# A new order of work between two attentions, and ScalarE copying both halves of the first attention's keys and values out of PSUM

## The reference, cut to what matters

```
h = rms_norm(x, attn_norm_w);  z = h @ w_in
c_q, c_kv, k_rope, dq, dk, dv, g_mla, g_diff = split_columns(z)
o_mla  = mla_attention(q(c_q), k(c_kv, k_rope), v(c_kv))          # 16 heads
o_diff = diff_attention(norm(dq), norm(dk), dv, lam, alibi)        # 8 heads, a1 - lam * a2
o_diff = rms_norm(o_diff, diff_subln_w) * (1 - lam_init)           # per head of 128
merged = sigmoid(g_mla + b) * o_mla + sigmoid(g_diff + b) * o_diff
x = x + merged @ w_out
x = x + expert_choice_moe(rms_norm(x, ffn_norm_w), ...)            # 16 experts
```

## Time and profile before

| | |
|---|---|
| median of the runs | 1512.5 us |
| the profiled execution: its time, and its span from the first to the last instruction | 1515.71 us, 1514.0 us |
| PE busy | 1162.2 us (77%) |
| DVE, ACT, POOL busy | 510.4, 373.4, 48.9 us |
| chain that ended last | DMA 53%, PE 39%, DVE 5%, ACT 1% |
| granted PE clock, mean | 0.88 of full speed |

### The profile page before, as it was taken

One profiled execution on the slowest core, in us unless ns is written; L12 is line 12 of the kernel. 1 busy time (PEld: TensorE's weight loads), 2 busy tenths in 40 slices (PEclk: granted clock), 3 DMA queues, 4 the chain that ended last, 5 costly groups with the idle time before them and its releaser, 6 DMA issues.

```text
span 1514.0 us, 19783 instructions
## 1 busy us (share of the span) xinstructions
PE 1162.2 (77%) x8185; PEld 693.2 (46%) x8185; DVE 510.4 (34%) x945; ACT 373.4 (25%) x616; POOL 48.9 (3%) x78
## 2 busy tenths in 40 slices
PE   9999899876557666566666666666665999999998
PEld 8877688422112112112122122122121778999887
DVE  6998866311011011011010010110110568665546
ACT  5658444300001001000000000100100463465434
POOL 2000350000000000000000000000000000000000
PEclk9999989997888678878788687788878999999999
DMA  8553516899999999999999999999999662555551
GB/s 299 195 210 129 197 36 249 359 427 426 426 427 426 426 429 427 428 428 427 428 428 427 428 428 428 428 427 427 429 427 427 248 213 101 182 174 194 183 181 53
DMA packets 58616, 493.31 MB, mean 326 GB/s; under 512 B 6666, under 2 KB 8260, under 8 KB 33988
## 3 DMA queue, kind: packets, MB, share of 16 engines
q1 hardware_dynamic: 57620, 491.54, 79.7%
q10 hardware_dynamic: 944, 1.05, 0.2%
HBM read 491.52 MB, written 1.05 MB: 325 GB/s over the span
## 4 chain that ended last, share of the span: by engine, by line
DMA 53%; PE 39%; DVE 5%; ACT 1%; issue 1%; SPq 0%; ACTq 0%; DVEq 0%; POOL 0%; POOLq 0%
DMA arena<-in_expert_w_down 18%; DMA arena<-in_expert_w_up 18%; DMA arena<-in_expert_w_gate 17%; PE ps L1831 11%; PE ps L1922 7%; PE ps L1836 6%; PE ps L2267 4%; DVE w_split L1126 2%; PE ps L2285 1%; PE ps L2113 1%; PE ps L2084 1%; PE ps L1901 1%; PE ps L1805 1%; PE ps L2344 1%; PE ps L2096 1%
## 5 line engine op out<-in xcount | busy, mean ns | idle before, releaser
L1126 DVE TENSOR_TENSOR w_split<-ring,w_split 128x1024 fp32r<-128x1024 f32 (+3 forms) x178 | 205.1, 1159 | 106.0 <-ACT w_split L710 104.6
L2267 PE MATMUL ps<-ring,arena 128*32 128x512 f32 x1024 | 162.8, 774 | 95.7 <-DMA ring<-in_expert_w_up 66.1
L2267 PE MATMUL ps<-arena 128*32 128x512 f32 x1024 | 164.0, 784 | 86.9 <-DMA arena<-in_expert_w_up 59.2
L710 ACT ACTIVATE w_split<-ring 128x1024 fp32r<-128x1024 f32 (+3 forms) x178 | 175.3, 990 | 199.2 <-PE ps L1836 139.9
L1567 DVE TENSOR_TENSOR arena<-arena,ps 128x512 f32<-128x512 f32 x16 | 11.0, 687 | 502.5 <-PE ps L2267 502.5
L1574 DVE TENSOR_TENSOR xs<-ps,xs 128x512 f32<-128x512 f32 x64 | 39.7, 682 | 289.7 <-PE ps L2293 289.7
L2267 PEld LDWEIGHTS ps<-ring,arena 128*32 128x32 f32 x1024 | 33.2, 130 | 217.3 <-DMA ring<-in_expert_w_up 105.4
L2267 PEld LDWEIGHTS ps<-arena 128*32 128x32 f32 x1024 | 33.5, 130 | 210.2 <-DMA arena<-in_expert_w_up 98.1
L1922 PE MATMUL ps<-hT_hi,w_split 128*128 128x256 f32 x608 | 112.7, 286 | 0.2 <-DVE arena L1738 0.2
L2285 PE MATMUL ps<-arena 128*32 128x256 f32 x1056 | 77.6, 442 | 37.7 <-DMA arena<-in_expert_w_down 34.8
L2285 PE MATMUL ps<-ring,arena 128*32 128x256 f32 x928 | 73.2, 470 | 38.9 <-DMA ring<-in_expert_w_down 35.2
(11 more groups left out here) (356 smaller groups left out, 1405.5 us busy)
## 6 DMA issues: line engine op xcount, KB each, us to landing
arena<-in_expert_w_gate SPq DMA_DIRECT2D x35, 2048.0 KB, 35.8
ring<-in_expert_w_up SPq DMA_DIRECT2D x35, 2048.0 KB, 36.4
ring<-in_expert_w_gate SPq DMA_DIRECT2D x29, 2048.0 KB, 37.0
arena<-in_expert_w_up SPq DMA_DIRECT2D x29, 2048.0 KB, 37.2
arena<-in_expert_w_down SPq DMA_DIRECT2D x25, 2048.0 KB, 33.8
ring<-in_expert_w_down SPq DMA_DIRECT2D x21, 2048.0 KB, 34.7
ring<-in_w_ff SPq DMA_DIRECT2D x32, 1024.0 KB, 5.0
ring<-in_w_in SPq DMA_DIRECT2D x24, 1024.0 KB, 5.0
```

The costliest lines, as they stand in the source:

```text
L710: act.activation(w_split[:, n % WBUFS, 0, 0:cols], slot_view(slot, cols)[:, n % 2, :], ACT.Copy).then_inc(split_hi, 1)
L1126: dve.tensor_tensor(buf[:, 1, :], w, buf[:, 0, :].bitcast(F32), ALU.subtract).then_inc(split_lo, 1)
L2267: m = pe.matmul(ps[j * CAP:(j + 1) * CAP, bank, :], xe[:, kt, :], w[:, r, j * FCOL:(j + 1) * FCOL], start=kt == 0, stop=kt == KT - 1, skip ...
```

## The change

It has these parts.

1. The second halves of dk and dv are copied by ACT right behind the first halves, and no longer by DVE.
2. In the last three steps of the first attention's loop (i = 9, 10, 11), PE transposes a head's probabilities ahead of the gate tile and computes the output behind it. The probabilities of heads 6 and 7 get banks of their own (5 and 6), and ACT's copies follow the same order.
3. The squares of the first attention's output move from POOL to ACT, and their sums from POOL to one DVE reduction, which stands before the low part of gate tile 15. POOL keeps roots and products. The product with the second gate moves from POOL to DVE, as four instructions (`gate_outputs`) in steps 11 to 14 of the second attention.
4. In the second attention, the transpositions of head 4 stand before `mla_probs(2)`; ACT does the high parts of the output weights and the second gate's tanh behind a head's exponentials rather than ahead of them, in other steps; DVE's low parts of the output weights come one step later, and the second gate's bias is added behind a head's work in steps 4 and 5. Head 6 waits for the first half of the bias only, and `mla_probs` for the second.

The core of the diff:

```diff
# POOL
-            pool.wait_ge(hO_evac, DHEADS)
-            pool.wait_ge(sq_read, 5)
-            for h in range(HALVES):
-                pool.tensor_tensor(xn[:, h, :], dq[:, h, :], dq[:, h, :], ALU.mult).then_inc(od_squares, 1)
-            pool.wait_ge(od_squares, HALVES)
-            squares = sq.rearrange("p (n d) -> p n d", d=DV)
-            width = DV // 2
-            while width:
-                total = squares[:, :, 0:width] if width > 1 else ss_o.unsqueeze(2)
-                step(pool.tensor_tensor(total, squares[:, :, 0:width], squares[:, :, width:2 * width], ALU.add))
-                width //= 2
+            pool.wait_ge(od_sum, 1)
...
-            for c in range(2):
-                cols = slice(c * D // 2, (c + 1) * D // 2)
-                pool.wait_ge(gate_ready, HALVES + c + 1)
-                step(pool.tensor_scalar(gb[:, :, cols], gb[:, :, cols], 1.0, None, ALU.add))
-                pool.tensor_tensor(dq[:, :, cols], gb[:, :, cols], dq[:, :, cols], ALU.mult).then_inc(od_gated, 1)
+            pool.sem_inc(od_ready, 1)
# ACT
+            def evac_other_half(name, dst):
+                act.activation(dst, pset(SETS[name], 1), ACT.Copy, scale=rstd_0[:, 1:2]).then_inc(block_dve, 1)
...
             evac("dk", (dk[:, 0, :], whole))
+            evac_other_half("dk", dk[:, 1, :])
...
                     evac("dv", (dv[:, 0, :], whole))
+                    evac_other_half("dv", dv[:, 1, :])
                     gate_high(2)
-                if i >= 4:
+                if i > DHEADS:
+                    diff_probs(i - 3) if i < DHEADS + 3 else None
+                if 4 <= i <= DHEADS:
                     diff_output(i - 4)
...
-                if 3 <= i < DHEADS + 3:
+                if 3 <= i <= DHEADS:
                     diff_probs(i - 3)
+                if i > DHEADS:
+                    diff_output(i - 4)
...
+            act.wait_ge(hO_evac, DHEADS)
+            act.wait_ge(sq_read, 5)
+            for h in range(HALVES):
+                act.activation(xn[:, h, :], dq[:, h, :], ACT.Square).then_inc(od_squares, 1)
...
-                if i in (4, 6, 8):
-                    high_parts("out", (i - 4) // 2, (i - 2) // 2)
-                if i in (5, 7):
-                    c = (i - 5) // 2
...
+                if i in (3, 5, 7):
+                    high_parts("out", (i - 3) // 2, (i - 1) // 2)
+                if i in (6, 8):
+                    c = (i - 6) // 2
+                    g = gb[:, :, c * 512:(c + 1) * 512]
+                    act.wait_ge(gate_in, 4)
+                    act.activation(g, g, ACT.Tanh, scale=0.5).then_inc(gate_ready, 1)
# DVE
-            evac("dk", (dk[:, 1, :], whole))
...
-            evac("dv", (dv[:, 1, :], whole))
...
             key_scale(1)
+            dve.wait_ge(od_squares, HALVES)
+            dve.tensor_reduce(ss_o, sq.rearrange("p (n d) -> p n d", d=DV), AX, ALU.add).then_inc(od_sum, 1)
             gate_low(15)
...
+            def gate_outputs(c):
+                cols = slice(c * D // 4, (c + 1) * D // 4)
+                dve.wait_ge(od_ready, 1)
+                dve.wait_ge(gate_ready, HALVES + c // 2 + 1)
+                dve.scalar_tensor_tensor(dq[:, :, cols], gb[:, :, cols], 1.0, dq[:, :, cols], ALU.add, ALU.mult).then_inc(od_gated, 1)
-            out_after = {5: 0, 7: 1, 9: 2}
+            out_after = {6: 0, 8: 1, 10: 2}
...
+                if HEADS - 6 < i <= HEADS - 2:
+                    gate_outputs(i - HEADS + 5)
# PE
             def diff_probs(u):
                 pe.wait_ge(prob_ready, 2 * u + 2)
-                if u >= 1:
+                if u >= DHEADS - 2:
+                    pe.wait_ge(hS_read, 4 * DHEADS)
+                elif u >= 1:
                     pe.wait_ge(hO_evac, u)
...
-                if i >= 4:
+                if DHEADS < i < DHEADS + 3:
+                    diff_probs(i - 3)
+                if 4 <= i <= DHEADS:
                     diff_output(i - 4)
...
-                if 3 <= i < DHEADS + 3:
+                if 3 <= i <= DHEADS:
                     diff_probs(i - 3)
+                if i > DHEADS:
+                    diff_output(i - 4)
...
             mla_scores(3)
+            mla_transposes(4)
             mla_probs(2)
             mla_output(1)
-            for i in range(4, HEADS + 2):
+            for i in range(5, HEADS + 2):
```

26 lines of the change are left out of this document (14 added, 12 removed).

## The result

The changed kernel took 1504.22 us (median of 4 runs, 1503.60 to 1506.11) against 1512.52 us before: 8.3 us less, a ratio of 0.9949 with a 95% interval of 0.9931 to 0.9966. It is faster, by more than a measurement can tell from no change. The prediction said 1502.1 in a range of 1497.5 to 1508.5.

What follows compares the result with a forecast made beforehand. The engines, chiefly PE, bound the front, the expert weights' transfer the middle and PE the end. The terms +1.5 - 4.15 - 8.7 + 1.0 = -10.35 us took the median from 1512.5 to 1502.1, range 1497.5 to 1508.5.

Steps and rivals of the forecast that it cites:

- Part 1: Copies of dk and dv: ACT's sequential copies delay DVE's dk work and the first gate tile, +1.5 us (-0.5 to +2.2).
- Part 2: First attention's last three steps: three PE waits of 1.25 us go, worth nothing except letting DVE start earlier.
- Part 3: DVE's way to the second attention's first maximum: 25.70 us becomes 21.55, so -4.15 us (-1.5 to -6.1).
- Part 4: Second attention, scores of head 3 to head 8: 13.8 us for 22.54, so -8.7 us (-9.4 to -4).
- Part 5: Second gate's product as four DVE instructions in successive second-attention steps: +1.0 us (0 to +2.8).
- One for one: Assumption that a microsecond won or lost on PE in the front moves all that follows by the same amount.
- The signs: Expected in the profile after, such as heads 3 to 8 in 14 us and the experts' DMA full some 10 us earlier.
- R1: Second attention, heads 3 to 8: the clock falls again, costing about 3.5 us with its stall; 1506.5 us; chance 0.15.
- R2: Heads 10 to 15: DVE becomes the bound, costing 2.8 us plus 3.5 for a clock fall; about 1507.5; chance 0.09.
- R3: Second attention's loop turns ACT- and DVE-bound, PE stays at the low clock; slower than before, 1521 us; chance 0.04.
- R4: Before head 1's scores: another wait replaces DVE's, experts' stream starts only 0 to 2 us sooner; 1511.5; chance 0.06.

Runs made afterwards that it cites:

- the repeat: The changed kernel run again unaltered, for a second profile of it; 1504.89 us, ratio 0.9948.
- the second profile: The kernel before run again unaltered, for another profile of it; this execution took 1512.65 us.
- experiment 6: Changed kernel with the old order inside the second attention on TensorE, ScalarE and VectorE; 1508.91 us, ratio 0.9977.
- experiment 8: Changed kernel with both the old order inside the second attention and the second gate's product on GpSimd; 1508.24 us, ratio 0.9975.
- experiment 9: Kernel before with only the second gate's product moved from GpSimd to VectorE; 1512.88 us against 1512.05, ratio 1.0003.
- experiment 7: Changed kernel with the second gate's product on GpSimd again, VectorE's four instructions gone; 1509.03 us, ratio 0.9973.
- experiment 3: Changed kernel with the second halves of dk and dv copied by VectorE again; 1504.62 us, ratio 0.9947.
- experiment 5: Changed kernel with squares and sums of the first attention's output on GpSimd again; 1511.60 us, ratio 0.9991.
- experiment 10: Changed kernel with 12 more matmuls on TensorE between gate tile 13 and head 1's scores; 1504.74 us, ratio 0.9947.
- experiment 11: Changed kernel with VectorE's sum of squares behind the second attention's first maximum and gate tile 15's low part behind the second; 1502.42 us, ratio 0.9931.

## Why the prediction was right, and where it was not

The direction, the places and the mechanism hold; the gain was 8.3 us for 10.35, because part 4 was priced too high.

**Part 1**, +1.5: the profiles with and without it differ by 1.7 us at the attention's end. Right.

**Part 2**, worth nothing but VectorE's earlier start: right as to VectorE (2.2 us), but it is worth 0.5 us at the end and not 2.3, because without it the clock didn't fall behind head 1 in the one profile taken.

**Part 3**, -4.15: VectorE's way took 21.44 us for the 21.55 predicted, and head 1's scores came 2.5 us sooner with part 1's 1.7 against them. Right. GpSimd's gating of the first gate kept its toll, as I had left it: it cost VectorE 1.6 us in the repeat and 1.5 before. The squares on ScalarE took 2.01 us in the repeat, with no table load and no wait of TensorE. What part 3 is worth now is more, since undoing it costs 4.8 us. The clock fell behind head 1 as expected.

**Part 4**, -8.7, is the term that was mis-sized. The 13.8 us forecast for the new order came out as 14.19, with one stall of 0.41 us for 0.3. But the 22.54 us of before were those of one execution: in the second profile they were 19.22. The first held a chain of chances: a fall of the clock that ended early, TensorE then ahead of VectorE's low part, which GpSimd's product held to 3.20 us, a stall of 1.59 us, a second fall. I noted that the execution was 3.2 us above the median and still took the whole difference as gain. Against the second profile part 4's stretch gives 5.0 us. Of these, 2.0 us are the old order itself, without a fall: 16.21 us in all three other profiles with that order (experiments 6, 8, 9) against 14.19. The other 3.0 us are the fall of the clock behind the stall of 1.30 us, which both profiles of the kernel before have and those three lack, whether GpSimd does the product or not; they had a low clock behind head 1 that cost 1.1 to 1.5 us more. With the new order, which has no such stall, none of nine profiles falls there. What decides whether a fall follows the stall stays open. (One reading of mine was also wrong: in 228 to 232 us VectorE, 3.19 of 4.00 us, was busier than ScalarE, 2.28, so ScalarE was not the narrowest.)

**Part 5**, +1.0: from head 8's scores to the attention's end are 25.16 us with the product on VectorE, for 24.74 in the second profile before and 24.56 in experiment 8, so it costs 0.4 to 0.6 us: within the bounds, below the term. But that is against the product where it used to stand. In the new order it would meet VectorE's low parts, and with it on GpSimd the same stretch takes 26.32 us (experiment 7): there the move saves 1.2 us, which I left out.

**The sum.** -2.5 - 5.0 + 0.4 = -7.1 us at the attention's end; that is 3.2 short of the forecast. The measured 8.3 lies nearer to it by something outside the change: both profiles of the kernel before have a fall of the clock some 80 us into the second block that neither profile of the changed kernel has, 1.4 us (329.7 and 329.6 us from that block's start to the last instruction, for 328.3 and 328.2). How much of the medians' 8.3 is of this kind isn't known. "One for one" holds: from the attention's end to the second block are 937.9 to 938.3 us in 11 of 14 profiles, both kernels among them, and 1.4 to 2.5 more in the three where the clock fell again behind it.

**The signs** that the prediction listed are in the rows: no idle time before the last outputs, 1.54 us instead of 0.49 where VectorE's dk work comes later, head 1's scores at 185.09 with 3.3 us of idle time and a low clock, no slow low part, 14.2 us at clock 1.00. One more was off: the experts start 7.1 us earlier, not 10; what the attention gained arrived whole.

**The rivals.** R1 (low clock again in heads 3 to 8) didn't come: 1.00 from 192 us on. Its premise, that any stall of 1.3 to 1.6 us is followed by the low clock, held in the traces that I had; in experiments 6, 8 and 9 the stall of 1.30 us wasn't. R2 neither: a last idle time of 0.59 us is all that part 5 left. R3 and R4 are out by the time.

**What stays open.** Medians and profiles disagree in experiments 3, 5, 7, 9, 10 and 11 by 1 to 3 us. Falls of the clock at places outside the change (front, start of the experts, second block), some 1.5 us each and 0 to 3 in an execution, are large enough to make this, and I have counted them in one execution each. Why some kernels meet more of them on the average wasn't settled.

## What to carry to other kernels

Before pricing a stretch from one profile, see how far that execution lies above the median, and take a second profile of the kernel before: a fall of TensorE's clock in it is a loss that most executions may not have. GpSimd's `tensor_tensor` work held VectorE's low parts until the instruction beside them was over, so its price depends on what it meets in time: the same squares and additions cost VectorE 4.1 us in one placement and 7.1 in another. Moving them off paid (6.7 us in the median of experiment 5); moving the product alone did not (experiment 9), so the toll can't be read from the old placement. What stands ahead of the first result that the next engine needs should be moved behind it, one instruction at a time, before anything is moved to another engine.

## What the runs showed of the hardware

- The low clock needs no idle time that the profile shows: in experiment 7, TensorE was busy 4.00 of 4.00 us at clock 1.00 in 1232 to 1236 us, and the clock fell in the next 4 us (mean 0.71).
- A stall of 1.30 us before head 4's scores was followed by the low clock in both profiles of the kernel before and not in those of experiments 6, 8 and 9 (scores of 1.96 and 2.02 us for 1.10).
- The same idle time of 1.7 us in the front was followed by a fall in 3 of 13 profiles; one fall costs about 1.5 to 1.9 us.
- A low clock that lasts longer can cost less: in the second profile before, TensorE stayed low until 211 us and met no stall behind it, while in the first it rose at 208 us, ran into VectorE's late work and fell again, 3 us worse.
- A VectorE low part that starts within GpSimd's product ends 1.1 us after it; beside GpSimd's `tensor_scalar` of 2.77 us it keeps its 1.21 us. The Trainium skill (SBUF — State Buffer, "Who interferes with whom") has a VectorE instruction with two SBUF inputs contend with any GpSimd instruction that reads SBUF: the product agrees (2.26 us for 1.22), this `tensor_scalar` doesn't. The two of the first gate, 2.23 us together, do: two VectorE instructions beside them in the repeat took 1.28 and 1.14 us for 0.42.
